# The w_out product of a two-block transformer layer as three rounded passes instead of one float32 product

## The chip, the cores and the metric

One core of one Trainium2 chip. The metric is the device time of one execution, in microseconds (us): the median of several runs.

## The reference

Two blocks follow one another on 512 tokens of width 1024, all in float32. Of the first block this case concerns its middle: four mixers (attention `a`, windowed attention `b`, a pooling mix, a long convolution) each give 256 channels, and these are joined, multiplied by `w_out` and added to the residual. Then come a norm, a router, 16 experts of which each token takes two, and the final norm of the block. The second block begins with another norm and a projection `w_in`.

```python
xl = xl + g1_l * (jnp.concatenate([a_l, b_l, p_l, h_l], axis=-1) @ lp['w_out'])
hl2 = rmsnorm(xl, lp['norm2_g']) * (1.0 + sc2_l) + sh2_l
y = moe(hl2.reshape(B * S, D), router_w, router_b, lp['moe_w1'], lp['moe_w3'], lp['moe_w2'])
xl = xl + g2_l * y.reshape(B, S, D)
...
x = rmsnorm(xl, final_g)            # end of block one
h = rms_norm(x, norm_gain[l])       # start of block two
proj = jnp.einsum('bsd,de->bse', h, w_in[l])
```

## The kernel before

The residual `xT` lies with channels on the partitions: 8 parts `k` of 128 channels, each 512 tokens wide. The joined mixers lie the same way in `mixT`, which is the first 512 columns of `hT`: parts 0 and 1 come from attention `a`, 2 and 3 from `b`, 4 and 5 from the pooling, 6 and 7 from the convolution. `arena` is one large scratch buffer whose regions change hands; `ring` has three slots of 2 MB for weights.

Every engine has its own program, written out by hand; they meet at semaphores. What PE fills and others read goes through four pairs of PSUM banks, taken in turn by *units* in one fixed order (`units_of_block_one`, `units_after_moe`). A unit names the engine that empties its banks (`act` or `dve`); PE may start a unit only once the unit four places earlier is emptied (`start_unit`, `banks_free`).

*The loop of attention b* (`turns`, L96; PE from L2851, ACT from L1239, DVE from L2036) goes through 16 pairs of query tile and head. In turn i PE transposes the probabilities of i-1 (`t`, L2865), makes the scores of i+1 (`s`, a split product in three passes) and the output of i-1 (`o`, L2602). DVE adds the bias (L1963) and takes the maximum (L1964), ACT makes the exponential (L1249) and copies the transposed probabilities (L1267), in the order exp(i+1), copy of t(i). Behind every fourth pair `ot` transposes the outputs (L2845), and ACT copies them into `mixT` (L1219). At i = 12 the outputs of attention a are transposed as well (L2882, copy L1277).

*After the loop* comes the unit `pm`: two float32 products of 512 columns for the pooling mix, which ACT scales into `mixT` (L1289). Then `w_out(j)` for j = 0 to 3 (L2890): two output parts each, for each part 8 float32 products of a 128x128 weight block by 512 columns. All float32 and rounded products of a helper are recorded at L2602 (`products`). DVE adds each part to the residual (L2072), ACT squares it (L1314). Between them stand `sr` and `rc` (small products for the router's shift), fed by 16 small copies on ACT (L1295), and the router's sums of squares (`route_sums`, L2914). ACT splits the first experts' weights into high parts (`moe_high`, L1309) and DVE makes the low parts (`moe_low`, L2064), in the gaps.

*A split product* runs in three passes: each operand x is written as a rounded copy hi (type float32r, made by ACT) and the rest lo = x - hi (made by DVE, in place of x); PE then sums w_hi·x_hi, w_hi·x_lo and w_lo·x_hi. The experts (L2992 to L2994), the second block's `w_in` (`in2_unit`, L3120 to L3122) and others are computed so already; `w_out` is not.

*Experts.* There are 17 tiles in this execution. The routing ends in a product that makes the list of tokens by tile (`list`). GpSimd gathers 128 token rows for each tile by an indirect DMA (L1011), PE transposes them (L2986), ACT and DVE split them (L1357, L2236), and PE goes through w1, w3 and, one tile behind, w2. SP loads expert weights of 2 MB each. After the first gather (`s_taken`, 16 for each) it issues w1 of tile 1, w2 of tile 0 and w3 of tile 1 (L848 to L851), and from then on each load waits until its slot has been split. ACT writes each tile's result to memory (L1341, L1343). At the end GpSimd gathers two rows for each token back (L1033).

*Final norm of block one and norm of block two.* DVE adds the experts' results (L2291), ACT squares (L1406), and PE sums the squares with two weightings: for each k and each of 4 token tiles one product with the squares as the weights and 2 columns moving (L3080), 64 in all. From the sums DVE, ACT and DVE make two factors for each token (L2303 to L1687), DVE spreads them onto diagonals (L2310) and PE broadcasts them (`n4`, `nx`).

`load(n)` on SP, for a slab of `w_in` from the fourth on (n = 22 and 23), first waits for the unit that last used its slot:

```python
if earlier and not N_BEFORE_OUT <= n < N_BEFORE_MOE + RING:
    filled(sp, last_unit[SLABS[earlier[-1]]])
```

For n = 22 that unit is `("q", 1)`, the second unit of the `w_in` product.

## Time and profile before

| what | value |
|---|---|
| median of 3 runs | 1423.01 us (1418.47 to 1431.56) |
| the profiled execution, own time | 1431.44 us |
| its span in the profile | 1429.6 us |
| PE busy | 1291.4 us, 90% of the span |
| DVE busy | 835.5 us, 58% |
| ACT busy | 572.8 us, 40% |
| mean granted clock of PE | 0.943 of full speed |

Times in the profile count from the start of the span. PE is TensorE, PEld its weight loads, DVE is VectorE, ACT is ScalarE, POOL is GpSimd, SP is SyncE. L12 is line 12 of the kernel before. A float32 product shows as two records, a rounded one as one.

### The profile page before, as it was taken

What the parts mean: (1) busy time and instruction counts of PE and PEld (TensorE: products, weight loads), DVE (VectorE), ACT (ScalarE), POOL (GpSimd) and SP (SyncE); (2) the same over time, 40 slices, a digit from 0 to 9 for tenths busy, and PEclk for the clock granted to TensorE, in tenths of its full rate; (3) what the DMA queues carried; (4) which work ended last, traced back from release to release, by engine and by line L of the source; (5) the groups of instructions that cost most, each with busy time, mean ns of one, the idle gap of its engine ahead of it and who ended that gap; (6) DMA issues with size and microseconds to landing.
All of it is one profiled execution on the core that took longest, in us unless ns stands there. A gap on an engine that the chain in (4) does not pass through costs nothing.

```text
span 1429.6 us, 16966 instructions
## 1 busy us (share of the span) xinstructions
PE 1291.4 (90%) x6478; PEld 927.3 (65%) x6478; DVE 835.5 (58%) x1241; ACT 572.8 (40%) x752; POOL 127.7 (9%) x126
## 2 busy tenths in 40 slices
PE   6999999988899899599999999589988898989796
PEld 2554456666768545478888788468867777765674
DVE  2347978736866205578888888454226456634444
ACT  1413000114545423267777777332324343334322
POOL 1100101000015000110122111100000000000000
PEclk9989999999999999699999999759998999889898
DMA  9523737565040030589999999722333454544201
GB/s 370 239 83 120 263 142 291 206 136 114 1 169 19 1 122 32 233 301 397 407 404 417 393 405 402 296 95 86 104 128 106 158 174 143 158 148 161 88 1 59
DMA packets 52838, 270.67 MB, mean 189 GB/s; under 512 B 15047, under 2 KB 22087, under 8 KB 38056
## 3 DMA queue, kind: packets, MB, share of 16 engines
q1 hardware_dynamic: 38280, 209.52, 39.7%
q0 software_dynamic: 9744, 47.19, 8.9%
q10 hardware_dynamic: 4752, 13.11, 2.3%
q8 instruction: 42, 0.69, 0.2%
q14 instruction: 20, 0.16, 0.0%
HBM read 229.42 MB, written 36.70 MB: 186 GB/s over the span
## 4 chain that ended last, share of the span: by engine, by line
PE 77%; DVE 10%; DMA 4%; ACT 4%; issue 4%; POOL 0%; SPq 0%; DVEq 0%; ACTq 0%; POOLq 0%
PE PS L2602 29%; PE PS L2992 7%; PE PS L2993 6%; PE PS L2994 6%; PE PS L3215 3%; PE PS L3216 3%; PE PS L3217 3%; PE PS L3121 2%; PE PS L3120 2%; PE PS L3122 2%; PE PS L3201 1%; PE PS L2865 1%; PE PS L2619 1%; PE PS L2986 1%; DMA arena<-stream_rows,arena 1%
## 5 line engine op out<-in xcount | busy, mean ns | idle before, releaser
L2602 PE MATMUL PS<-arena 128*128 128x64 f32 (+7 forms) x786 | 194.8, 414 | 24.6 <-DMA arena<-in_small_f_w 7.6
L1309 ACT ACTIVATE arena_r<-ring 128x2048 fp32r<-128x2048 f32 x100 | 185.9, 1910 | 18.4 <-DMA ring<-in_moe 11.8
L2602 PEld LDWEIGHTS PS<-arena 128*128 128x128 f32 (+2 forms) x786 | 119.7, 201 | 90.0 <-issue 67.6
L2602 PE MATMUL PS<-hT,ring 128*128 128x512 f32 (+1 forms) x432 | 175.1, 563 | 1.4 <-ACT hT L1289 1.4
L2064 DVE TENSOR_TENSOR arena_r<-ring,arena_r 128x2048 fp32r<-128x2048 f32 x66 | 148.2, 2287 | 21.2 <-ACT arena_r L1309 21.2
L2602 PEld LDWEIGHTS PS<-hT,ring 128*128 128x128 f32 x432 | 81.1, 190 | 92.3 <-issue 86.9
L3215 PE MATMUL PS<-arena_r 128*128 128x512 f32 x256 | 106.1, 415 | 16.7 <-DVE ring_r L2463 12.3
L2992 PE MATMUL PS<-arena_r,hT_r 128*128 128x512 f32 x272 | 112.2, 413 | 5.5 <-DVE hT_r L2236 4.9
L2993 PE MATMUL PS<-arena_r,hT_r 128*128 128x512 f32 x272 | 108.1, 398 | 0.0
L3217 PE MATMUL PS<-arena_r,ring_r 128*128 128x512 f32 x256 | 103.7, 405 | 0.0
L1160 ACT ACTIVATE arena<-PS 128x1024 f32<-128x1024 f32 (+2 forms) x31 | 28.5, 927 | 176.5 <-PE PS L2602 161.7
L2064 DVE TENSOR_TENSOR hT_r<-ring,arena_r 128x2048 fp32r<-128x2048 f32 x34 | 76.4, 2289 | 26.2 <-ACT arena_r L1309 26.1
L2463 DVE TENSOR_TENSOR ring_r<-ring,arena_r 128x1024 fp32r<-128x1024 f32 (+1 forms) x40 | 40.3, 1011 | 84.5 <-ACT arena_r L1452 83.9
L3216 PE MATMUL PS<-hT_r,arena_r 128*128 128x512 f32 x192 | 77.4, 403 | 0.0
L1773 DVE TENSOR_TENSOR arena<-arena 128x512 f32<-128x512 f32 (+2 forms) x104 | 71.9, 692 | 3.7 <-DVE arena L1815 0.2
L3215 PEld LDWEIGHTS PS<-arena_r 128*128 128x128 f32 x256 | 50.0, 195 | 35.7 <-issue 16.7
L2992 PEld LDWEIGHTS PS<-arena_r,hT_r 128*128 128x128 f32 x272 | 51.7, 190 | 21.7 <-DVE hT_r L2236 5.7
L2274 DVE TENSOR_TENSOR ring_r<-ring,arena_r 128x1024 fp32r<-128x1024 f32 x18 | 21.9, 1225 | 64.0 <-ACT arena_r L1400 64.0
L1452 ACT ACTIVATE arena_r<-ring 128x1024 fp32r<-128x1024 f32 (+1 forms) x40 | 35.3, 884 | 58.2 <-PE PS L3217 54.0
L2993 PEld LDWEIGHTS PS<-arena_r,hT_r 128*128 128x128 f32 x272 | 51.8, 190 | 10.4
L3217 PEld LDWEIGHTS PS<-arena_r,ring_r 128*128 128x128 f32 x256 | 50.0, 195 | 11.8
L2992 PE MATMUL PS<-arena_r 128*128 128x512 f32 x136 | 54.4, 400 | 2.8 <-DVE arena_r L2229 2.8
(428 smaller groups left out, 2308.0 us busy)
## 6 DMA issues: line engine op xcount, KB each, us to landing
ring<-in_moe SPq DMA_DIRECT2D x51, 2048.0 KB, 10.9
ring<-in_slabs SPq DMA_DIRECT2D x27, 2048.0 KB, 10.3
ring<-in_slabs SPq DMA_DIRECT2D x9, 1024.0 KB, 6.0
y_rows<-arena ACTq DMA_DIRECT2D x17, 512.0 KB, 10.0
ssm_scratch<-arena POOLq DMA_DIRECT2D x4, 1152.0 KB, 6.2
arena<-ssm_scratch POOLq DMA_DIRECT2D x4, 1152.0 KB, 9.0
arena<-in_tab_fwd SPq DMA_DIRECT2D x2, 2048.0 KB, 15.0
ssm_scratch<-arena POOLq DMA_DIRECT2D x4, 1024.0 KB, 10.3
```

Source lines behind the costliest of these rows:

```text
L1309: nc.scalar.activation(rounded(moe_w_hi[n][:, cols]), ring[:, n, cols], ACT.Copy).then_inc(s_moe_hi[n], 1)
L1452: nc.scalar.activation(rounded(w_hi[:, n % 2, 0:w.shape[1]]), w, ACT.Copy).then_inc(s_w_hi, 1)
L1773: then(nc.vector.tensor_tensor(out, x, y, op))
L2064: nc.vector.tensor_tensor(rounded(moe_w_lo[n][:, cols]), ring[:, n, cols], as_float(moe_w_hi[n][:, cols]), ALU.subtract).then_inc(s_moe_lo ...
L2463: nc.vector.tensor_tensor(rounded(w), w, as_float(w_hi[:, n % 2, 0:w.shape[1]]), ALU.subtract).then_inc(s_w_lo, 1)
L2602: ins = nc.tensor.matmul(out, lhsT, rhs, start=(n == 0), stop=(n == len(pairs) - 1))
L2992: nc.tensor.matmul(out, rounded(x_hi), rounded(w_hi_), start=first, stop=False)
L2993: nc.tensor.matmul(out, rounded(x_lo), rounded(w_hi_), start=False, stop=False)
L2994: return nc.tensor.matmul(out, rounded(x_hi), rounded(w_lo_), start=False, stop=last)
L3215: nc.tensor.matmul(out, w_h, x_h, start=(k == 0), stop=False)
L3216: nc.tensor.matmul(out, w_h, x_l, start=False, stop=False)
L3217: ins = nc.tensor.matmul(out, w_l, x_h, start=False, stop=(k == last))
```

## The change

It computes `w_out` as a split product in three passes. The four joined mixers are split in eight parts: ACT makes the high parts of 6, 7, 0 and 1 and of the first weight chunk inside the loop of attention b (`during_b`), the others after it; DVE follows with the low parts. The weights go in 8 chunks of 128 output channels through three buffers. The unit `pm` moves into the loop at i = 14. Other edits: SP waits for the second gather, not the first, before the loads of L848 to L851; SP waits for the last gather of results before the fourth and fifth slab of `w_in`; the first split of w3 moves on ACT behind the copies of the normed rows; at the end of the experts ACT copies the last tile's transposed gates ahead of the second but last result; the one-hot operands of `list` are rounded; the two sums of squares are made with 32-column weights and 512 columns moving, the roots taken from PSUM on 64 rows and transposed. Scratch regions of squares move, and semaphores are renamed.

```diff
@@ -111,6 +111,8 @@
             yield ("ot", i // HEADS - 1)
+        if a == "b" and i == 14:
+            yield ("pm",)
@@ -118,6 +120,8 @@
         return ("a", "ot"), "act"
+    if kind == "pm":
+        return ("pm",), "act"
@@ -147,7 +151,6 @@
             u += [((a, "ot", QT - 1), "act")]
-    u += [(("pm",), "act")]
@@ -239,7 +242,7 @@
     u = [(("y_tr", j), "dve") for j in range(4)]
-    u += [(("n3", 0), "dve"), (("n3", 1), "dve"), (("n4",), "dve"), (("nx",), "dve")]
+    u += [(("n3",), "act"), (("nt",), "dve"), (("n4",), "dve"), (("nx",), "dve")]
@@ -364,6 +367,21 @@
         o_a2 = region(R_HY, [QT, 256])
+        WO_CHUNKS, MIX_PARTS = 8, 8
+        mix_hi = region(R_HY + 1024, [KD, T])
+        wo_hi = [region(start, [KD, P]) for start in (R_HY, 0, 1024)]
+        def wo_weights(n):
+            w = slab(("w_out", n // 4)).rearrange("p (k c) -> p k c", k=KD)
+            return w[:, :, P * (n % 4):P * (n % 4) + P]
+        def wo_chunk_done(eng, n):
+            if n % 2:
+                filled(eng, ("wo", n // 2))
+            else:
+                eng.wait_ge(s_chunk_a, n // 2 + 1)
@@ -843,7 +862,7 @@
                 sp.dma_start(ring[:, 2], moe_d[bass.ds(3 * e + 2, 1)].rearrange("a p c -> p (a c)")).then_inc(s_moe_w[2], 16)
-            sp.wait_ge(s_taken, 16)
+            sp.wait_ge(s_taken, 32)
@@ -863,6 +882,7 @@
             sp.wait_ge(s_moe_y, tiles)
+            sp.wait_ge(s_back[QT - 1], 32)
@@ -1221,6 +1241,30 @@
                                      ACT.Copy).then_inc(s_act_read, 1)
+            def mix_high(k):
+                nc.scalar.activation(rounded(mix_hi[:, k]), mixT[:, k], ACT.Copy).then_inc(s_op_hi, 1)
+            def wo_high(n):
+                slab_here(act, ("w_out", n // 4))
+                if n >= 3:
+                    wo_chunk_done(act, n - 3)
+                nc.scalar.activation(rounded(wo_hi[n % 3]), wo_weights(n), ACT.Copy).then_inc(s_w_a_hi, 1)
+            def during_b(i):
+                if i in (9, 10):
+                    act.wait_ge(s_gate, 4)
+                    mix_high(i - 3)
+                elif i == 11:
+                    act.wait_ge(s_pool_d, 4)
+                    wo_high(0)
+                elif i in (13, 14):
+                    read(act, ("a", "ot"))
+                    mix_high(i - 13)
@@ -1271,6 +1315,13 @@
                             high_b(i)
+                        else:
+                            during_b(i)
+                    elif turn[0] == "pm":
+                        filled(act, key)
+                        for g in range(2):
+                            ins = nc.scalar.activation(mixT[:, 4 + g], bank(key, g), ACT.Copy, scale=V("pool_scale", g, g + 1))
+                        ins.then_inc(s_act_read, 1)
@@ -1283,21 +1334,22 @@
                     out_tr(a, QT - 1)
-            key = ("pm",)
-            filled(act, key)
-            for g in range(2):
-                ins = nc.scalar.activation(mixT[:, 4 + g], bank(key, g), ACT.Copy, scale=V("pool_scale", g, g + 1))
-            ins.then_inc(s_act_read, 1)
+            read(act, ("b", "ot", QT - 1))
+            for k in range(2, 6):
+                mix_high(k)
+            wo_high(1)
+            wo_high(2)
...
                 ins.then_inc(s_diags, 1)
+            wo_high(3)
...
             copy_unit(("rc",), rt_const, bank(("rc",), 0)[:, 0:EXPERTS])
+            wo_high(4)
@@ -1312,8 +1364,12 @@
                 nc.scalar.activation(sq_2[:, k], xT[:, k], ACT.Square).then_inc(s_sq, 1)
-                if k in (3, 5):
-                    moe_high((k - 3) // 2, 0, False)
+                if k == 1:
+                    wo_high(5)
+                    wo_high(6)
+                elif k == 3:
+                    wo_high(7)
+                    moe_high(0, 0, False)
@@ -1325,6 +1381,7 @@
                 copy_unit(("h_tr", t), h_rows[:, t], both(("h_tr", t)), rt_rstd[:, t:t + 1])
+            moe_high(1, 0, False)
@@ -1385,8 +1442,8 @@
                 nc.scalar.activation(rounded(moe_w_hi[0][:, cols]), ring[:, 0, cols], ACT.Copy).then_inc(s_moe_hi[2], 1)
+            gT_high(tiles - 1)
             moe_y_out(tiles - 2)
-            gT_high(tiles - 1)
...
-            root(4, nst[:])
+            act.wait_ge(s_gsq, 2)
+            filled(act, ("n3",))
+            nc.scalar.activation(root_rows[0:64], bank(("n3",), 0)[0:64], ACT.Sqrt, scale=1.0 / D,
+                                 bias=eps_n[0:64]).then_inc(s_act_read, 1)
...
                 act.wait_ge(s_h2, k + 1)
@@ -2034,6 +2094,18 @@
                                                 in1=V("norm2_g"), op0=ALU.add, op1=ALU.mult))
+            def wo_low(n):
+                dve.wait_ge(s_w_a_hi, n + 1)
+                w = wo_weights(n)
+                nc.vector.tensor_tensor(rounded(w), w, as_float(wo_hi[n % 3]), ALU.subtract).then_inc(s_w_a_lo, 1)
+            def mix_low(part):
+                dve.wait_ge(s_op_hi, part)
+                k = (6, 7, 0, 1, 2, 3, 4, 5)[part - 1]
+                nc.vector.tensor_tensor(rounded(mixT[:, k]), mixT[:, k], as_float(mix_hi[:, k]), ALU.subtract).then_inc(s_op_lo, 1)
@@ -2044,6 +2116,14 @@
                 norm_a(i)
+                if i == 12:
+                    wo_low(0)
+                elif i in (11, 13, 14, 15):
+                    mix_low({11: 1, 13: 2, 14: 3, 15: 4}[i])
+            for part in range(5, 9):
+                mix_low(part)
+            for n in range(1, 3):
+                wo_low(n)
@@ -2064,6 +2144,7 @@
                                             ALU.subtract).then_inc(s_moe_lo[n], 1)
+            wo_low(3)
@@ -2077,6 +2158,9 @@
                         ins.then_inc(s_x1, 1)
+                if j < 2:
+                    wo_low(2 * j + 4)
+                    wo_low(2 * j + 5)
@@ -2250,8 +2334,10 @@
                 nc.vector.tensor_tensor(moe_g, moe_s, PS[:, 1, :], ALU.mult).then_inc(s_moe_g, 1)
-            nc.vector.memset(gsq[:, :, 0:1], 1.0).then_inc(s_gsq, 1)
-            nc.vector.tensor_tensor(gsq[:, :, 1], V("final_g"), V("final_g"), ALU.mult).then_inc(s_gsq, 1)
+            then(nc.vector.tensor_tensor(gsq[:], V("final_g"), V("final_g"), ALU.mult))
+            nc.vector.tensor_scalar(gsq_32, gsq[:, :, None].broadcast_to([P, KD, 32]), EPS, None, ALU.add).then_inc(s_gsq, 1)
+            nc.vector.memset(eps_n[0:32], EPS * EPS)
+            nc.vector.memset(eps_n[32:64], EPS).then_inc(s_gsq, 1)
@@ -2296,16 +2382,11 @@
                         ins.then_inc(s_x2, 1)
-            for half in range(2):
-                key, tiles_of = ("n3", half), slice(2 * half, 2 * half + 2)
-                filled(dve, key)
-                sums = PS[:, 2 * U.slot(key):2 * U.slot(key) + 2, 0:2]
-                then(nc.vector.tensor_scalar(nst[:, 1, tiles_of], sums[:, :, 0], 1.0 / D, EPS, ALU.mult, ALU.add))
-                nc.vector.scalar_tensor_tensor(out=nst[:, 0, tiles_of], in0=nst[:, 1, tiles_of], scalar=EPS * D,
-                                               in1=sums[:, :, 1], op0=ALU.mult, op1=ALU.add).then_inc(s_dve_read, 1)
-                read(dve, key)
-            nc.vector.tensor_scalar(nst[:, 0], nst[:, 0], 1.0 / D, None, ALU.mult).then_inc(s_mean, 1)
-            inverse(4, nst[:])
+            key = ("nt",)
+            filled(dve, key)
+            nc.vector.reciprocal(nst[:], bank(key, 0)[:, 0:64 * QT].rearrange("p (t a c) -> p a t c", a=2, c=32)[:, :, :, 0]
+                                 ).then_inc(s_dve_read, 1)
+            read(dve, key)
@@ -2882,29 +2963,34 @@
                         ins.then_inc(s_filled, 1)
+                    elif turn[0] == "pm":
+                        start_unit(key)
+                        pe.wait_ge(s_pool_d, 4)
+                        for g in range(2):
+                            products(bank(key, g), [(pool_w[:, g], pool_d[:, g])], last=(g == 1))
...
                     out_tr(a, QT - 1)
-            key = ("pm",)
-            start_unit(key)
-            pe.wait_ge(s_pool_d, 4)
-            for g in range(2):
-                products(bank(key, g), [(pool_w[:, g], pool_d[:, g])], last=(g == 1))
...
                 start_unit(key)
-                if j == 0:
-                    read(pe, ("pm",))
-                    pe.wait_ge(s_gate, 4)
-                slab_here(pe, ("w_out", j // 2))
-                w = slab(("w_out", j // 2)).rearrange("p (k c) -> p k c", k=KD)
                 for c in range(2):
-                    col = 256 * (j % 2) + P * c
-                    products(bank(key, c), [(w[:, k, col:col + P], mixT[:, k]) for k in range(KD)], last=(c == 1))
+                    n = 2 * j + c
+                    hi, lo = wo_hi[n % 3], wo_weights(n)
+                    first, then_ = (6, 7, 0, 1), (2, 3, 4, 5)
+                    passes = [[(w, x, k) for k in ks] for w, x, ks in ((hi, mix_hi, first), (hi, mixT, first), (hi, mix_hi, then_),
+                                                                      (hi, mixT, then_), (lo, mix_hi, first + then_))]
+                    pe.wait_ge(s_w_a_hi, n + 1)
+                    for m, (w, x, k) in enumerate(sum(passes, [])):
+                        if n == 0 and m in (0, 4, 8, 12):
+                            pe.wait_ge(s_op_lo if m % 8 else s_op_hi, 4 if m < 8 else 8)
+                        if m == 2 * KD:
+                            pe.wait_ge(s_w_a_lo, n + 1)
+                        ins = nc.tensor.matmul(bank(key, c), rounded(w[:, k]), rounded(x[:, k]), start=(m == 0), stop=(m == 3 * KD - 1))
+                    ins.then_inc(s_filled if c else s_chunk_a, 1)
@@ -3071,16 +3157,19 @@
                 ins.then_inc(s_filled, 1)
-            for half in range(2):
-                start_unit(("n3", half))
-            pe.wait_ge(s_gsq, 2)
+            start_unit(("n3",))
+            pe.wait_ge(s_gsq, 1)
...
                 pe.wait_ge(s_sq, 3 * KD + k + 1)
-                for t in range(QT):
-                    ins = nc.tensor.matmul(bank(("n3", t // 2), t % 2)[:, 0:2], sq[:, k, P * t:P * t + P], gsq[:, k],
-                                           start=(k == 0), stop=(k == KD - 1))
-                    if k == KD - 1 and t % 2:
-                        ins.then_inc(s_filled, 1)
+                for n, w in enumerate((gsq_32[:, k], ones[:, 0:32])):
+                    ins = nc.tensor.matmul(bank(("n3",), 0)[32 * n:32 * n + 32, :], w, sq[:, k, 0:T], start=(k == 0), stop=(k == KD - 1))
+            ins.then_inc(s_filled, 1)
+            key = ("nt",)
+            start_unit(key)
+            read(pe, ("n3",))
+            for t in range(QT):
+                ins = nc.tensor.transpose(bank(key, 0)[:, 64 * t:64 * t + 64], root_rows[0:64, P * t:P * t + P], ident[0:64, 0:64])
+            ins.then_inc(s_filled, 1)
...
```

## Rows read from the trace of the kernel before

**Rows 1.** The page, part 4: the chain that ended last, shares of the span by line
```profile
PE PS L2602 29%; PE PS L2992 7%; PE PS L2993 6%; PE PS L2994 6%; PE PS L3215 3%; PE PS L3216 3%; PE PS L3217 3%; PE PS L3121 2%; PE PS L3120 2%; PE PS L3122 2%; PE PS L3201 1%; PE PS L2865 1%; PE PS L2619 1%; PE PS L2986 1%; DMA arena<-stream_rows,arena 1%
```

**Rows 2.** Stretches: us, busy (count) of PE, PEld, DVE, ACT, POOL; granted clock; DMA share; GB/s
```profile
core 0: us, PE busy (x) PEld busy (x) DVE busy (x) ACT busy (x) POOL busy (x), PEclk, DMA share, GB/s
486.00:488.00 2.00, 2.00 (x5) 0.97 (x6) 0.76 (x5) 0.38 (x1) 0.00 (x0) 0.54 0.02 4
613.00:903.00 290.00, 289.35 (x1344) 235.13 (x1345) 250.28 (x143) 222.70 (x158) 46.44 (x30) 1.00 0.97 391
948.00:950.00 2.00, 2.00 (x11) 2.00 (x11) 0.00 (x0) 0.00 (x0) 0.00 (x0) 0.50 0.00 0
973.20:1062.50 89.30, 89.30 (x389) 72.37 (x388) 26.61 (x28) 26.33 (x28) 1.06 (x2) 1.00 0.26 84
```

**Rows 3.** Timeline of PE, end of loop b to w_out: start, us, line, count, idle before
```profile
465.05 1.52 PE L2602 MATMUL PS<-arena 128*128 128x64 f32 x12 [0.28 <-ACT arena L1267]
...
480.44 1.52 PE L2602 MATMUL PS<-arena 128*128 128x64 f32 x12 [1.46 <-ACT arena L1267]
...
486.15 3.58 PE L2602 MATMUL PS<-arena 128*128 128x512 f32 x4
491.13 13.97 PE L2602 MATMUL PS<-hT,ring 128*128 128x512 f32 x32 [1.40 <-ACT hT L1289]
```

**Rows 4.** Timeline of ACT, one turn of loop b, and the evacuation of pm
```profile
464.11 0.80 ACT L1267 ACTIVATE arena<-PS 128x768 f32<-128x768 f32 x1
...
489.76 1.26 ACT L1289 ACTIVATE hT<-PS,vec 128x512 f32<-128x512 f32 x2 [3.03 <-PE PS L2602]
```

**Rows 5.** Groups by shape on ACT and DVE, whole run: count, busy us, mean ns
```profile
L1400 ACT ACTIVATE arena_r<-ring 128x1024 fp32r<-128x1024 f32 x18 | 18.8, 1055 | 32.0 <-PE PS L3122 23.3 <-PE PS L3105 8.1 <-ACT arena L1341 0.6
...
L1410 ACT ACTIVATE arena_r<-hT 128x512 fp32r<-128x512 f32 x8 | 5.1, 632 | 4.3 <-DVE hT L2315 4.1
...
L2274 DVE TENSOR_TENSOR ring_r<-ring,arena_r 128x1024 fp32r<-128x1024 f32 x18 | 21.9, 1225 | 64.0 <-ACT arena_r L1400 64.0
```

**Rows 6.** The chain in order of time, 440 to 1120 us: start, us, what
```profile
577.33 3.59 PE PS L2602 x16
...
590.95 11.46 DMA arena<-stream_rows,arena
...
941.31 13.80 PE PS L3080 x64
```

**Rows 7.** DMA issues in short stretches: KB each, us from issue to landing
```profile
arena<-stream_rows,arena POOLq DMA_INDIRECT x1, 5.6
...
ring<-in_moe SPq DMA_DIRECT2D x1, 2048.0 KB, 17.8
...
ring<-in_moe SPq DMA_DIRECT2D x1, 2048.0 KB, 7.7
```

**Rows 8.** Timelines of SP, ACT and PE around the second tile
```profile
588.43 0.37 SPq L848 DMA_DIRECT2D ring<-in_moe  x1
...
599.98 3.70 ACT L1309 ACTIVATE arena_r<-ring 128x2048 fp32r<-128x2048 f32 x2
...
613.04 0.50 PE L2992 MATMUL PS<-arena_r,hT_r 128*128 128x512 f32 x1 [2.43 <-DVE hT_r L2236]
```

**Rows 9.** Timeline of ACT and PE around the last expert_out
```profile
905.09 0.60 ACT L1348 ACTIVATE arena_r<-PS 128x512 fp32r<-128x512 f32 x1 [0.56 <-ACT arena L1341]
...
906.63 0.79 PE L2992 MATMUL PS<-arena_r 128*128 128x512 f32 x1 [2.83 <-DVE arena_r L2229]
```

**Rows 10.** Timelines and groups around the two norms' sums
```profile
939.04 1.34 ACT L1406 ACTIVATE arena<-xT 128x512 f32<-128x512 f32 x2 [19.10 <-DVE xT L2291]
...
956.28 1.29 DVE L2310 TENSOR_TENSOR arena<-ident,nst 128x512 f32<-128x512 f32 x2
...
558.31 0.44 PE L2955 MATMUL PS<-ident,arena 64*128 64x64 f32 x4 [0.87 <-DVE arena L2086]
...
L1318 ACT ACTIVATE arena<-PS,arena 32x512 f32<-32x512 f32 x1 | 0.7, 680 | 0.1
```

49 lines of the change are left out of this document (25 added, 24 removed).

## The prediction, made before the changed kernel ran

> **What bounds the kernel now.** I read the page's chain first, then stretches with their granted clock, then the timeline of each place that the diff touches. The chain is mostly PE, and its largest line is L2602, the helper through which the float32 products go, w_out's among them [rows 1]. The changed places are therefore on the path, or hold it up. Four matter.
>
> The tail of loop b and w_out: PE makes pm in 3.58 us at about half clock, waits for ACT's two copies and starts w_out at 491.13, in units of 13.97 us [rows 2, 3]. The list: 16 short records take 3.59 us [rows 6]. The experts: PE is busy 289.35 of 290 us at full clock with DMA at 0.97, so inside the loop there is nothing to win and little to spare; only its start (a second gather of 11.46 us, a restart of PE at 613.04) and its end (906.63) are loose [rows 2, 6, 8, 9]. The norm sums: 64 products with 2 columns take 13.80 us while the clock stands at 0.50 [rows 2, 6].
>
> **The product itself.** Before: 4 x 13.97 = 55.9 us [rows 3]. After: 8 chunks x 8 blocks x 3 = 192 passes of 512 columns. The w_in product makes 16 chunks of 24 passes in 89.30 us; about 0.6 us of that are transposes, so a pass takes 88.7/384 = 0.231 us [rows 2]. 192 x 0.231 = 44.4 us: 11.5 us less. It is on the path, since nothing behind it can start before the residual parts.
>
> **pm moved.** From 486.15 to 491.13 PE does nothing but pm and wait: 5.0 us go from the tail [rows 3], since the first eight passes need only parts that the loop has already split. In the loop pm costs PE 3.58/2 = 1.8 us at full clock; its copies (1.26 us on ACT [rows 4]) stand beside t(14) and replace a wait of 1.46 us before o(14) [rows 3]. If that cover is missing they cost 1.3 us more.
>
> **Splits in the loop.** ACT gets four copies of 0.63 us and one of 1.05 us [rows 5]. They stand between an exponential and the copy of t(i), for which PE waits: copy at 464.11, PE at 465.05 after 0.28 us idle [rows 3, 4]. So they are not free. The one at i = 10 costs 0.6 us. The one at i = 11 is swallowed, since the exponential of that turn was not delayed by the earlier shift. The weight chunk at i = 12 costs 1.05 us. Those at i = 14 and 15 lie under pm and under a wait. Together 1.7 us; between 0 and 3.6 us (all five exposed). Queued behind them on ACT are the copies of t(i), and behind these PE. DVE's low parts come after its output of the turn, in a wait for scores.
>
> **The start of w_out.** After the last ot ACT must copy it (0.38 us in the profile) and split four parts, 2.5 us. PE meanwhile makes eight passes. pm ran at 3.58/8 = 0.45 us a pass at that place, and the tail's waits stay as they are, so I count the eight at half clock: 8 x (0.45 - 0.23) = 1.8 us lost, and the four parts arrive just in time. At full clock they would take 1.8 us and PE would wait some 1.1 us: nearly the same.
>
> **The feed of the later chunks.** High part 1.05 us, low part 1.23 us [rows 5], chunk 24 x 0.231 = 5.5 us, three buffers. Chunk n+3's high part waits for chunk n, so it has two chunks, 11 us, to be ready. Queued in front of wo_high(3) are the 16 diagonal copies (4.9 us), in front of wo_high(4) sr's and rc's copies. By my order of time, with w_out starting at 0, wo_low(3) ends near 16 and chunk 3 starts near 22; chunk 4 starts near 29, its low part ends near 19; chunk 7's low part waits for chunk 4 and ends near 37, chunk 7 starts near 48. Nothing waits, and the first w1 split comes behind wo_high(7) with its load then landed. If all of the feed were exposed: 8 x 2.3 = 18 us.
>
> Net of these parts: 11.5 + 5.0 - 1.8 - 1.7 - 1.8 = 11.2 us.
>
> **The list.** Rounded operands make 8 passes of 16 records: 3.59/2 = 1.8 us less [rows 6], and the first gather waits for it. No row shows a rounded product of 24 columns; bounds 0 and 2.5 us.
>
> **Loads after the second gather.** Alone, a gather lands in 5.6 us; the second, beside three loads, took 11.46 [rows 6, 7]. PE waited 3.0 us for it, so this wait goes. What is late next is w1 of tile 1: the loads leave near 597.3 instead of 588.43 [rows 8]. A load with the queue to itself lands in 7.7 us [rows 7], so at 605.0. Then half a high split (1.9), two low splits (4.5), the gate product (0.7) and the low part of the taken rows (1.2) follow on ACT and DVE, and PE restarts at 613.4 against 613.04 [rows 8]. I take 0. Bounds: 3 us won if loads and gather are each faster; 4 us lost if w1 takes as long as the row allows, 599.98 - 588.43 = 11.5 us [rows 8]. By tile 2 the delay is gone, since DMA stands nearly idle between 609 and 626 in the profile. The Trainium skill says (DMA: Bandwidth & Descriptors, "Queues, rings and completion order") that completion is not in order of issue within one issuing engine. The last of the three loads landed after 17.8 us [rows 7]; if w1 landed only then, PE would restart some 10 us later. The trace speaks for order of issue: w1's split started with no wait at 599.98.
>
> **The end of the experts.** gT_high now precedes the result copy and can start 1.2 us sooner than 905.09 [rows 9], but PE also needs the copy (1.0 us) behind it: PE starts at about 905.7 instead of 906.63, 0.9 us. It runs its first passes at 0.43 us there; should the shorter gap keep the clock up, 3 us more. Bounds 0 and 4.
>
> **Norm sums.** Now 16 float32 products of 512 columns, two side by side for each k. Per k: 4 passes, 1.8 us at half clock (0.45 each), 0.92 at full. The first square is ready near 939.7 [rows 10]. Elsewhere wide products bring the full clock after some 3.5 us (pm at half clock, w_out behind it at full) [rows 2, 3]; so two k at 1.8 and six at 0.92 end at 948.8. Squares come every 0.75 us and do not hold it. Then a root (0.68), four transposes (0.44), a reciprocal (0.2): diagonals at 950.3 instead of 956.28 [rows 10], 6.0 us. If the clock stays low: 8 x 1.8, ending at 954.1, and 0.7 us are won. Best case 7.5. The Trainium skill (TensorE: Matmul & The Clock Gate, "What's actually happening") says that the array is throttled by default and that being busy releases it. The row disagrees for the old sums: PE busy 2.00 of 2.00 us at 0.50 [rows 2]. [...]
>
> **At nothing.** The first w3 split moves to ACT behind the row copies, where ACT is idle from 574 to 590, and DVE wants it near 580; without that cover 3.7 us, still before w3's use at 604. SP's wait for the result gathers delays nothing: the two loads behind it already wait for ("q", 1), long after. So that edit does not do what it says, and the result gathers stay as they are.
>
> **Sum.** 11.2 + 1.8 + 0 + 0.9 + 6.0 = 19.9 us. The profiled execution: 1431.4 - 19.9 = 1411.5. It lies at the upper end of the three runs; their median is 1423.0, so the time is 1403. A measurement tells about 1% (14 us) from no change, so "faster" begins below 1409.
>
> **Rivals.**
> - *All loose ends fall well* (clock kept at the expert end, splits hidden, gather gain kept): 19.9 + 1.7 + 1.5 + 3 + 3 + 0.5, about 30 us, 1393. For it: each wait is short. Against: they are independent. Chance 0.12.
> - *The clock stays low in the norm sums, and w1 comes late*: 5.3 + 4 us less gain, about 1412. For it: the clock stood at 0.50 for this whole stretch; against: pm. 0.14 for either of them in full.
> - *The w_out feed is exposed*: PE waits for each chunk's split in the hand-written queues of ACT and DVE: 18 us back, 1421. Against: 11 us of lead. 0.05.
> - *Slower: the experts become paced by DMA.* DMA is at 0.97 [rows 2], and the loads start 9 us later. If the lead is never regained, every tile waits. It decides from 19.9/15 = 1.3 us a tile; at 2 us for 15 tiles it costs 30 us, 1433. Against: the idle DMA stretch at the start, and a split loop that needs less than the 18.1 us of a tile. 0.04.
>
> My forecast itself, within 6 us: 0.65. It leaves 1397 to 1409. Down to 1391 most of the first rival is in, up to 1413 the second; outside remain the last two and the tails. Faster: 0.65 + 0.12 and about half of the second, 0.84; the same: 0.12; slower: 0.04.
>
> **What would show it.** w_out chunks of 5.5 us with no wait for ACT or DVE but in the first; pm at half its time in the loop; o(10) and o(12) later by 0.6 and 1.0 us; the second gather near 5.6 us, PE restarting within 1 us of the old distance; wide norm sums of about 9 us with the clock rising within them. Chunks above 6 us, a tile above 18.3 us, or norm sums above 13 us would make the forecast wrong.

## The result, and the profile after

The changed kernel took 1417.63 us, the median of 20 runs (1411.66 to 1429.75); 20 runs of the kernel before (the three of the table among them) gave 1428.04 (1418.47 to 1438.4). The ratio is 0.995 (0.9929 to 0.9972). That is 7 us less by the ratio and 10.4 by the medians: a gain, but one within 1%. The forecast was 1403 us, within 1397 to 1409, or 1391 to 1413 with its nearest rivals; the time lies above both ranges. "Faster" was to begin below 1409 and had a chance of 0.84; what came is what the forecast called "the same", at 0.12. The profiled execution took 1416.47 us with a span of 1414.6 (before 1431.44 and 1429.6).

The chain has w_out in a line of its own now: L2992 holds 3%, and the float32 helper, which is L2683 in the new file, 26% instead of 29% [rows 1]. The page of the changed kernel, part 4, shares of the span by line:

```profile
PE PS L2683 26%; PE PS L3078 7%; PE PS L3079 6%; PE PS L3080 6%; PE PS L2992 3%; PE PS L3304 3%; PE PS L3305 3%; PE PS L3306 3%; PE PS L3210 2%; PE PS L3209 2%; PE PS L3211 2%; PE PS L2946 1%; PE PS L3290 1%; PE PS L2700 1%; PE PS L3072 1%
```

A chain of shares doesn't say where the rest of the gain went, so I laid the two profiled executions side by side, from marker to marker (lengths in us; a marker is the start of the row named):

| stretch | before | after | gain | forecast |
|---|---|---|---|---|
| loop b: first output transpose, ot(0), to the last, ot(3) | 34.36 | 44.35 | -10.0 | -3.5 |
| tail and w_out: ot(3) to the row sums behind w_out's last chunk | 67.91 | 54.29 | +13.6 | +14.7 |
| list: to the first tile's row transposes | 33.91 | 32.13 | +1.8 | +1.8 |
| start of the experts: to the first gate transposes | 31.02 | 32.91 | -1.9 | 0 |
| experts: first to last gate transposes | 284.47 | 283.52 | +1.0 | 0 |
| end of the experts: to the last result copy | 12.19 | 12.36 | -0.2 | +0.9 |
| last result copy to the first square | 23.64 | 23.50 | +0.1 | 0 |
| norm sums: first square to the diagonals | 17.24 | 11.39 | +5.9 | +6.0 |
| together | | | +10.3 | +19.9 |

The two executions lie 15.0 us apart. The missing 4.7 are outside the table, 1.6 ahead of ot(0) and 3.1 behind the diagonals; such stretches differ from one execution to the next by more than that (below). What has to be explained is 10.3 where 19.9 were forecast, and two thirds of the gap stand in the first line: loop b became 10 us longer.

The timeline of PE in loop b of the changed kernel, 455 to 500 us (start, length, line, count, idle before and what ended it):

```profile
463.92 1.52 PE L2683 MATMUL PS<-arena 128*128 128x64 f32 x12 [0.79 <-ACT arena L1311]
...
473.02 1.67 PE L2683 MATMUL PS<-arena 128*128 128x64 f32 x12 [1.20 <-ACT arena L1311]
474.48 1.49 PE L2946 MATMUL PS<-ident,arena 128*128 128x128 f32 x6
475.90 2.29 PE L2683 MATMUL PS<-arena_r,hT_r 64*128 64x512 f32 x6
478.12 6.34 PE L2683 MATMUL PS<-arena 128*128 128x64 f32 x16
...
486.61 1.60 PE L2683 MATMUL PS<-arena 128*128 128x64 f32 x12 [1.41 <-ACT arena L1311]
...
490.91 2.79 PE L2683 MATMUL PS<-arena 128*128 128x64 f32 x12 [0.99 <-ACT arena L1311]
494.25 0.66 PE L2926 MATMUL PS<-ident,post 128*128 128x128 f32 x2 [0.54 <-DVE post L2054]
494.56 2.05 PE L2992 MATMUL PS<-arena_r 128*128 128x512 f32 x4
...
498.12 1.11 PE L2992 MATMUL PS<-arena_r 128*128 128x512 f32 x4
```

The two waits are the ones forecast: 0.79 us ahead of o(10), 1.20 ahead of o(12), where the same place had 0.25 to 0.28 before [rows 3]. What the forecast did not have is the column of lengths behind the second one. Six transposes (L2946) take 1.49 us there and 0.82 in an earlier turn (465.50); the group of 16, which is o(13) and pm together, takes 6.34. The stretches of the changed kernel around it (us, busy and count of PE, PEld, DVE, ACT, POOL; granted clock; DMA share; GB/s):

```profile
440.00:473.00 33.00, 30.10 (x213) 25.83 (x211) 22.00 (x39) 18.29 (x33) 11.94 (x9) 1.00 0.00 1
473.00:476.00 3.00, 2.98 (x19) 2.67 (x19) 2.04 (x5) 0.99 (x2) 0.00 (x0) 0.71 0.00 0
476.00:484.00 8.00, 8.00 (x22) 5.56 (x23) 2.78 (x6) 2.32 (x4) 0.00 (x0) 0.50 0.00 0
484.00:488.00 4.00, 2.59 (x19) 2.13 (x18) 0.00 (x0) 2.48 (x4) 0.00 (x0) 0.93 0.00 0
488.00:498.00 10.00, 8.47 (x32) 7.26 (x32) 3.22 (x8) 4.22 (x8) 0.00 (x0) 0.50 0.01 2
```

The granted clock is 1.00, which is 2.4 GHz, until 473, and falls to 0.50, which is 1.2 GHz, within three microseconds of the wait of 1.20. It stays there through eight microseconds in which PE is busy without a break, and again in the tail. In the kernel before the loop ran at 1.00 to its last turn, and the clock was low only behind it, in the tail [rows 2].

Who made PE wait is seen on ACT (same columns as for PE, timeline of ACT of the changed kernel):

```profile
469.33 0.90 ACT L1293 ACTIVATE arena<-PS,stat 128x768 f32<-128x768 f32 x1 [1.95 <-DVE stat L2024]
...
470.22 1.05 ACT L1254 ACTIVATE arena_r<-ring 128x1024 fp32r<-128x1024 f32 x1
471.17 1.01 ACT L1328 ACTIVATE hT<-PS 128x1024 f32<-128x1024 f32 x1
472.07 0.80 ACT L1311 ACTIVATE arena<-PS 128x768 f32<-128x768 f32 x1
```

L1254 is the rounded copy of w_out's first chunk. It stands between the exponential and the copy of the transposed probabilities (L1311), and so does a copy that this one turn has anyway, that of attention a's transposed outputs (L1328, which was L1277 before). With that copy alone PE waited 0.25 us here; with both it waits 1.20.

At the start of the experts the chain of the changed kernel, 560 to 960 us, reads (start, length, what):

```profile
575.37 5.25 DMA arena<-stream_rows,arena
580.67 1.98 PE PS L3072 x8
...
583.90 4.02 DMA arena<-stream_rows,arena
588.68 8.56 DMA ring<-in_moe
597.26 1.92 ACT arena_r L1361
...
601.42 2.28 DVE arena_r L2144
...
604.30 1.15 DVE hT_r L2320
...
899.41 10.03 DMA y_rows<-arena
...
933.73 7.71 PE PS L3165 x32
941.51 1.28 ACT L1466
942.81 0.69 ACT rstd L1466
```

The second gather now lands in 4.02 us instead of 11.46 [rows 6], as asked for; but the chain goes on through the load of w1, which left only at 588.68. While w1 was loaded and split PE stood idle for 5.74 us, and it restarted at 605.49 (timeline of PE of the changed kernel):

```profile
605.49 0.79 PE L3078 MATMUL PS<-arena_r,hT_r 128*128 128x512 f32 x1 [5.74 <-DVE hT_r L2320]
```

The granted clock is at 0.50 there (a stretch of the changed kernel, in the columns of the stretches above):

```profile
605.50:608.00 2.50, 2.50 (x6) 2.02 (x7) 0.00 (x0) 0.00 (x0) 0.00 (x0) 0.50 0.94 380
```

The end of the experts runs through a store of 10.03 us. The norm sums take 7.71 us instead of 13.80 [rows 6].

### The profile page after: what moved, and what is told of

Its sections match the earlier page's. It is cut to its first block, busy times and chain, and to the rows that moved or that the text cites. A ratio compares the mean times of both kernels' runs of the same rounds, so it can differ in the third digit from the quotient of the medians.

```text
span 1414.6 us, 17056 instructions
## 1 busy us (share of the span) xinstructions
PE 1273.6 (90%) x6506; PEld 930.1 (66%) x6506; DVE 849.2 (60%) x1254; ACT 585.3 (41%) x768; POOL 126.4 (9%) x126
## 4 chain that ended last, share of the span: by engine, by line
PE 77%; DVE 9%; DMA 5%; ACT 5%; issue 4%; POOL 1%; SPq 0%; POOLq 0%; DVEq 0%; ACTq 0%
PE PS L2683 26%; PE PS L3078 7%; PE PS L3079 6%; PE PS L3080 6%; PE PS L2992 3%; PE PS L3304 3%; PE PS L3305 3%; PE PS L3306 3%; PE PS L3210 2%; PE PS L3209 2%; PE PS L3211 2%; PE PS L2946 1%; PE PS L3290 1%; PE PS L2700 1%; PE PS L3072 1%
## 5 line engine op out<-in xcount | busy, mean ns | idle before, releaser
L2683 PE MATMUL PS<-arena 128*128 128x64 f32 (+6 forms) x770 | 189.0, 412 | 21.3 <-ACT arena L1311 8.9
L2683 PEld LDWEIGHTS PS<-arena 128*128 128x128 f32 (+2 forms) x770 | 116.8, 200 | 84.6 <-issue 61.5
L3078 PE MATMUL PS<-arena_r,hT_r 128*128 128x512 f32 x272 | 113.0, 416 | 8.2 <-DVE hT_r L2320 8.2
L2683 PE MATMUL PS<-hT,ring 128*128 128x512 f32 (+1 forms) x304 | 119.2, 550 | 0.0
L3304 PE MATMUL PS<-arena_r 128*128 128x512 f32 x256 | 105.1, 410 | 15.5 <-DVE ring_r L2544 11.3
L3079 PE MATMUL PS<-arena_r,hT_r 128*128 128x512 f32 x272 | 109.3, 402 | 0.0
L2683 PEld LDWEIGHTS PS<-hT,ring 128*128 128x128 f32 x304 | 57.1, 190 | 59.0 <-issue 56.6
L3080 PE MATMUL PS<-arena_r,hT_r 128*128 128x512 f32 x136 | 55.3, 407 | 0.0
```

Source lines behind the costliest of these rows:

```text
L2683: ins = nc.tensor.matmul(out, lhsT, rhs, start=(n == 0), stop=(n == len(pairs) - 1))
L3078: nc.tensor.matmul(out, rounded(x_hi), rounded(w_hi_), start=first, stop=False)
L3079: nc.tensor.matmul(out, rounded(x_lo), rounded(w_hi_), start=False, stop=False)
L3080: return nc.tensor.matmul(out, rounded(x_hi), rounded(w_lo_), start=False, stop=last)
L3304: nc.tensor.matmul(out, w_h, x_h, start=(k == 0), stop=False)
```

## The experiments

Each experiment edits the changed kernel, most in one place (x5 in two, x8 in three), and the measure is the stretch of the table in which the edit stands; whole times of single runs are told only where they matter. The first run is the changed kernel itself, on the chip and in the session of the next three.

**The changed kernel once more (x0_again).**

> The changed kernel once more, unaltered. From the transposes of ot(0) to those of ot(3) it took 44.4 us, against 34.4 before the change; 3.5 us more were forecast. Theory A (the splits in front of the copy of t(i) open a gap on PE of 1.2 us at i = 12, and the clock falls behind it): the fall comes at the same place again, near 474, and the stretch takes 43 to 45 us. Theory B (the fall was chance in one execution): the clock stays at 1.00 to about 486 and the stretch takes about 38 us.

Measured: loop b 44.21 us (44.35), ot(0) to the end of w_out 98.59 (98.64), start of the experts 33.16 (32.91), end 11.99 (12.36), norm sums 11.46 (11.39). In these two executions a stretch repeats within 0.4 us. Over all the runs below, where no edit touches them, loop b stays within 0.5 us (44.21 to 44.72 in six traces) and the start of the experts within 0.7 (32.72 to 33.37 in nine), but the list varies by 2.3 us (30.95 to 33.23), the end of the experts by 1.4 (11.20 to 12.57) and the norm sums by 2.0 (10.80 to 12.84). So single runs tell differences above 0.7 us in the first two stretches, and only larger ones in the others. The time of this run was 1414.37.

**The splits behind the copy that PE waits for (x1_after_copy).**

```
     # ACT, loop b: exponential | copy of probT (the "t" turn) | "o" turn
     (copy of probT, L1311)
+    if a == "b":
+        during_b(i)
...
-    else:
-        during_b(i)
```

> The five splits of the loop stand behind the copy of t(i) on ACT, where ACT waits 1.6 to 2.2 us for the maximum, instead of in front of it. Theory A: PE sees no new gap, the clock holds until pm is done, ot(0) to ot(3) takes 36 to 37 us (34.4 and pm at 1.8), w_out's chunks are unchanged, the kernel is 6 to 8 us faster than the changed one (ratio to the kernel before about 0.988). Theory C (pm's two wide products in the loop bring the clock down or are the cost themselves): the stretch stays at 43 us or more, with the clock at 0.50 from pm on, and the time stays as it is.

Measured: loop b 37.85 us, to the end of w_out 92.61 (98.64), a median of 1409.04 us in 4 runs and a ratio of 0.989 (0.982 to 0.996) to the kernel before. The splits themselves are all still there, in the same turns; one place further on in ACT's queue they cost PE nothing, and the loss from them was 6.5 us, not 1.7. (Theory A had named 36 to 37 us; the clock of the tail, below, took the rest.) The timeline of PE of this kernel:

```profile
473.54 1.52 PE L2683 MATMUL PS<-arena 128*128 128x64 f32 x12 [0.25 <-ACT arena L1311]
476.90 3.33 PE L2683 MATMUL PS<-arena 128*128 128x64 f32 x16
482.38 1.52 PE L2683 MATMUL PS<-arena 128*128 128x64 f32 x12 [1.49 <-ACT arena L1311]
486.20 2.80 PE L2683 MATMUL PS<-arena 128*128 128x64 f32 x12 [0.99 <-ACT arena L1311]
```

The wait ahead of o(12) is back at 0.25, and the group of 16 takes 3.33 us. The clock now falls only behind the 1.49 us wait of the tail, and o(15) pays 1.3 us for it.

**pm back in the tail (x2_pm_tail).** The rival theory for the long group was pm itself, since it is new in the loop.

```
     # order of the units
-    if a == "b" and i == 14: yield ("pm",)
...
+    u += [(("pm",), "act")]          # behind ot(3)
```

> pm stands behind the loop again, the splits stay in front of the copy of t(i). Theory A: the gap of 1.2 us at i = 12 is there, the clock falls behind it though pm is gone; ot(0) to ot(3) takes 39 to 41 us. Theory C: without pm in the loop the clock holds to about 486, the stretch takes 36 us (34.4 and 1.7 of gaps). In both pm costs 3.5 us at the tail, and w_out's first eight passes run beside its copies.

Measured: loop b 42.24 us, to the end of w_out 100.45. Without pm in it the loop is still 7.9 us longer than before, and the wait of 1.20 us ahead of o(12), which ends at 477.79, is followed by the half clock again: 0.69 from 477 to 482 and 0.50 from there. So pm isn't what brings the clock down. The loop came out longer than the 39 to 41 us of theory A, since the clock stayed at 0.50 through all its last turns. Moved back it costs 1.8 us more over the whole stretch.

**No splits in the loop at all (x3_splits_late).**

```
-    else:
-        during_b(i)
...
+    for i in (9, 10, 11, 13, 14):    # after the last ot, ahead of mix_high(2)
+        during_b(i)
```

(DVE's low parts follow them.)

> All splits stand behind the loop, pm stays in it. Theory A: no new gap before pm, so ot(0) to ot(3) takes 36 to 37 us; w_out starts 2 to 4 us after ot(3), since ACT must first make four parts and a weight chunk (0.4 + 2.5 + 1.05 us) and DVE the low parts; up to w_out's end it is 3 to 5 us shorter than the changed kernel. Theory C: the stretch stays at 43 us or more.

Measured: loop b 36.16 us, which is 34.36 + 1.80: pm costs what was forecast, to the hundredth. But w_out then waits 3.58 us for its first parts, and to its end it is 94.58, two microseconds worse than with the splits in the loop but behind the copy. That is what they are worth in the loop in these two runs, in both of which the eight first passes ran at half clock.

**Which of the five splits it is (x9_weights_in_front, x10_parts_in_front).** In the first only the weight chunk (1.05 us) stays ahead of the copy, in the second only the four parts (0.62 us each).

```
x9:   +  if a == "b" and i not in (11,): during_b(i)            # behind the copy
      -  else:                                      # at the "o" turn
      +  elif i in (11,):
x10:  +  if a == "b" and i not in (9, 10, 13, 14): during_b(i)
      -  else:
      +  elif i in (9, 10, 13, 14):
```

> Of the five splits only the weight chunk at i = 12 (1.05 us) stands in front of the copy, the four of 0.63 us behind it. Theory A (one gap of about 1.2 us on PE is enough for the clock to fall): ot(0) to ot(3) takes 42 to 44 us, the clock at 0.50 from about i = 13. Theory D (only several gaps in a row do it, the sum counts): the clock holds, 39 us.

> The reverse: the four parts stand in front of the copy, the weight chunk behind it. Theory A: gaps of at most 0.8 us, the clock holds, 38 to 39 us. Theory D: the clock falls here too, 42 us or more.

Measured: 41.61 and 36.48 us. The timeline of PE with the weight chunk in front:

```profile
477.41 1.52 PE L2685 MATMUL PS<-arena 128*128 128x64 f32 x12 [1.19 <-ACT arena L1311]
482.26 6.35 PE L2685 MATMUL PS<-arena 128*128 128x64 f32 x16
```

and with the four parts in front:

```profile
464.86 1.52 PE L2685 MATMUL PS<-arena 128*128 128x64 f32 x12 [0.80 <-ACT arena L1311]
...
476.38 3.32 PE L2685 MATMUL PS<-arena 128*128 128x64 f32 x16
```

One instruction carries most of it. Where no split delays PE and the clock holds, the loop takes 36.16 us (x3 and x8). The part at i = 10 costs 0.55 us of waiting (0.80 against 0.25), of which the stage loses 0.3. The weight chunk costs 0.94 us of waiting (1.19 against 0.25) and lengthens the loop by 5.4 us, three of them in the group of 16 alone. (Theory A had 42 to 44 us here, and 38 to 39 for x10; both came out shorter.) With all five in front, the changed kernel loses 8.2: of what is left, 2.2 us are a second fall of the clock in the last turns, which x9 doesn't have and x1 has without the wait of 1.2 us (ot(2) to ot(3) is 6.25 us in the changed kernel, 4.10 in x9, 5.79 in x1). Over all profiles of this study: with the wait of 1.2 us ahead of o(12) the clock fell right behind it in 8 of 8 (the changed kernel, x0, x2, x4 to x7, x9), without it the loop kept 1.00 through o(13) in 5 of 5 (before, x1, x3, x8, x10).

**The loads behind the first gather again (x4_first_gather).**

```
-    sp.wait_ge(s_taken, 32)
+    sp.wait_ge(s_taken, 16)
```

> Only SP's wait is undone: the three loads leave after the first gather again. Measured from the transposes of the first gathered tile to the first transposes of gates it was 31.0 us before the change, 32.9 and 33.2 in two executions with it. Theory A (w1 of tile 1 lands late, PE idles 5.7 us and restarts at half clock): 31.0 us, the second gather back at 11 us, PE waits 3 us for it. Theory B (the late loads cost nothing, the 1.9 us come from elsewhere): 32.9 us as with the change.

Measured: start of the experts 29.80 us (32.91). The chain of this kernel:

```profile
576.25 11.71 DMA arena<-stream_rows,arena
588.00 1.10 PE PS L3072 x8
```

The second gather takes 11.71 us again and PE waits 2.24 us for it. Yet the stage is 3.1 us shorter than with the wait in place (31.0 were expected): the weights leave 7.9 us earlier, 5.4 us behind the first gather's issue instead of 13.3, and PE's idle time is split in two waits, 2.24 and 2.43 us, instead of one of 5.74. PE restarts only 0.7 us sooner (24.10 us behind the first transposes, for 24.82), but at full clock, and is then 5.70 us from the gates instead of 8.09:

```profile
597.11 0.50 PE L3078 MATMUL PS<-arena_r,hT_r 128*128 128x512 f32 x1 [2.43 <-DVE hT_r L2320]
```

The wait bought a fast gather with a late w1, and that was a bad exchange, mostly through the clock. This run took 1398.79 us, but some 7 us of that belong to no edit: its ot(0) stands at 442.7 us, that of the changed kernel at 449.9.

**Only w1 ahead of the second gather (x7_w1_first).**

```
-    sp.wait_ge(s_taken, 32)
+    sp.wait_ge(s_taken, 16)
     (load of w1)
+    sp.wait_ge(s_taken, 32)
     (loads of w2 and w3)
```

> Only w1 of tile 1 leaves after the first gather, w2 and w3 wait for the second. Theory A: the second gather then shares DMA with one load and lands after 6 to 9 us, w1 lands 8 to 9 us after its issue, before PE needs it; PE waits 1 us or less for the gather; from the transposes of the first tile to the first gates 29 to 31 us. Rival: the gather is as slow beside one load as beside three (11 us), 31 us or more; or w3 of tile 1 now comes last and PE waits for it, 32 us.

Measured: 27.23 us, 5.7 less than the changed kernel and 3.8 less than the one before, a larger gain than I had expected. The timelines of SP, POOL and PE:

```profile
581.27 0.37 SPq L867 DMA_DIRECT2D ring<-in_moe  x1
583.80 0.98 POOL L1032 DMA_INDIRECT arena<-stream_rows,arena  x1 [0.81 <-POOL arena L1042]
590.17 0.34 SPq L869 DMA_DIRECT2D ring<-in_moe  x1
...
602.11 0.50 PE L3079 MATMUL PS<-arena_r,hT_r 128*128 128x512 f32 x1 [2.43 <-DVE hT_r L2321]
```

w1 leaves 7.4 us sooner. PE doesn't wait for the gather (its transposes follow a pass without a gap, at 593.05), and it restarts with the short wait of 2.43 us that the first tile has too. It also restarts at a full clock, at 0.23 us a pass (0.43 in the changed kernel, where it had stood idle for 5.7 us).

**The order at the end of the experts undone (x5_undo_order).**

```
-    sp.wait_ge(s_back[QT - 1], 32)
...
     moe_y_out(tiles - 2)
+    gT_high(tiles - 1)
     moe_y_out(tiles - 1)
```

(gT_high stood ahead of both result copies.)

> Two edits undone that should be worth nothing: SP's wait for the last result gather, and ACT's order at the end of the experts. From the last transposes of gates to the copy of the last result it was 12.2 us before the change, 12.4 and 12.0 with it. Theory A (the last copy waits for the store of the result before it, which takes 10 us): within 0.6 us of 12.2 again. Theory B (PE's earlier start counts): 13 us, 0.9 more. The result gathers: 14 to 15 us from first issue to last landing in any case, since the two loads behind SP's wait come later anyway; if the wait did something, they would take 2 us or more longer.

Measured: end of the experts 12.45 us (12.36), result copy to first square 23.35 (23.50). Neither part shows a difference, though for the first, with 11.20 to 12.57 in the other kernels with the new order, one of some tenths can't be excluded. The timeline of ACT says why. The changed kernel:

```profile
897.73 0.60 ACT L1405 ACTIVATE arena_r<-PS 128x512 fp32r<-128x512 f32 x1 [2.45 <-PE PS L3094]
898.22 1.02 ACT L1398 ACTIVATE arena<-PS 128x1024 f32<-128x1024 f32 x1
899.41 0.34 ACTq L1400 DMA_DIRECT2D y_rows<-arena  x1
909.46 1.02 ACT L1398 ACTIVATE arena<-PS 128x1024 f32<-128x1024 f32 x1 [10.21 <-DMA y_rows<-arena]
```

PE does start its last product sooner: 899.37 is 2.27 us behind the gate transposes, where 906.63 [rows 9] was 3.42 us behind them. But there is one buffer for results, so the last copy waits for the store of the copy before it, which left at 899.41 and took 10.03 us. Before, PE ended that wait (9.72 us, to 915.40, the store having landed at 914.78); now the store does.

**The table of the root loaded early (x6_root_table).**

```
     act.wait_ge(s_gsq, 2)
+    nc.scalar.activation(stat[0:64, 7, 7:8], eps_n[0:64], ACT.Sqrt)
     filled(act, ("n3",))
```

> One more square root of a single column ahead of ACT's wait for the sums, so that the table for roots is loaded before them. With the change the load of 1.28 us stood between the sums and the root, from the first square to the diagonals it was 11.4 to 11.5 us. Theory: 10.1 to 10.3 us. Rival: the table is not needed sooner, something else on ACT or PE ends last: 11.4 us.

Measured: norm sums 10.08 us (11.39, and 10.80 to 12.84 in the kernels without this edit; x8 below repeats it with 10.09). The timeline of ACT:

```profile
939.74 1.28 ACT L1465 ACT_TABLE_LOAD   x1
941.03 0.20 ACT L1465 ACTIVATE stat<-stat 64x1 f32<-64x1 f32 x1
942.24 0.68 ACT L1467 ACTIVATE rstd<-PS,stat 64x512 f32<-64x512 f32 x1 [1.01 <-PE PS L3166]
```

The load of 1.28 us now lies beside the last sums. PE, which waits 0.86 us for the root instead of 2.20, also makes the four broadcasts behind it in 1.95 us instead of 3.65.

**The three together (x8_three_mended): x1, x7 and x6 in one kernel.**

> Three edits on the changed kernel together: the loop's splits behind the copy of t(i), w1 of tile 1 alone after the first gather, the root's table loaded early. Alone they shortened their stretches by 6.5 us (loop), 5.3 us (start of the experts) and 2.2 us (norms to the first product of w_in). If they add up: 14 us less than the changed kernel, a ratio to the kernel before of about 0.983. Rival: the earlier end of one stage is lost in the next (a load then comes late): 0.988 or above.

Measured: 1397.46 us in 6 runs (1392.19 to 1404.73) against 1428.77 for the kernel before in 11, a ratio of 0.9804 (0.975 to 0.9858). It beats the kernel before, and, as its interval lies below the changed kernel's (0.9929 to 0.9972), that one too, though the two were not run side by side. Loop b 36.16, to the end of w_out 89.82, start of the experts 27.59, norm sums 10.09: 8.8 + 5.3 + 1.3 us below the changed kernel, 15.4 in all. The medians of the two kernels lie 20.2 us apart. Of the difference 0.8 us is the faster broadcast behind the diagonals; the other 4 us are in no stretch that these edits touch, and the two medians are from different chips. The timeline of PE in its tail:

```profile
479.52 3.32 PE L2685 MATMUL PS<-arena 128*128 128x64 f32 x16
...
484.99 1.52 PE L2685 MATMUL PS<-arena 128*128 128x64 f32 x12 [1.49 <-ACT arena L1312]
...
488.39 1.52 PE L2685 MATMUL PS<-arena 128*128 128x64 f32 x12 [0.99 <-ACT arena L1312]
...
490.62 1.18 PE L2994 MATMUL PS<-arena_r 128*128 128x512 f32 x4
...
493.56 1.19 PE L2994 MATMUL PS<-arena_r 128*128 128x512 f32 x4 [0.83 <-ACT arena_r L1247]
```

Here the clock stayed at 1.00 through the whole tail, the first eight passes took half their time, and PE then waited 0.83 us for the four parts that ACT splits after the last ot: the two cases that the prediction called nearly the same. The waits of 1.49 and 0.99 us are those of x1, behind the first of which it fell. x10 held its clock here too. So the fall in the tail is not settled by these waits alone; what decides between the two stays open.

## Why the prediction was wrong

The forecast held in most of its terms and failed in one, with two small misses beside it.

- **Failed: "Splits in the loop", "together 1.7 us".** The waits were right: 0.79 us ahead of o(10), 1.20 ahead of o(12), and against the 0.25 that x1 has there this is 1.5 us in all. The splits at 14 and 15 cost nothing, as said. But the step counted a wait on PE at its own length. Behind the wait of 1.20 us the clock fell, and that was the larger part: of the loop's 10.0 us, 1.8 are pm (x3), 1.5 the waits, and the other 6.7 the half clock. About 5.0 of these go with the splits (6.5 us between the changed kernel and x1, less the 1.5 of waits), and about 1.7 are a fall in the last turns that x1 has as well (37.85 against 36.16), so they are not shown to come from the splits. x9 and x10 put the first fall on one instruction, the weight chunk. The sentence "between 0 and 3.6 us (all five exposed)" excluded the truth, because its upper end was a sum of durations. I had read the clock of the tail [rows 2], so the way in which waits and clock hang together was in view; I never asked it of the stretch in which I was adding a wait. The Trainium skill has the shape of this (TensorE: Matmul & The Clock Gate, "A second HAM failure mode: psum-queue depth-cycling"): idle moments between groups of matmuls can be frequent enough that the clock goes down and up. The traces here agree that short waits can do it, with 18 of the 22 us from 476 to 498 at 0.50; what they add is that one wait of 1.20 us (x9: 1.19) was followed by the fall, where the page speaks of frequent ones.
- **Right: the product, pm, the start of w_out, the feed.** The three-pass product needs 11.34 us for a pair of chunks (524.01 to 535.35 in the timeline of PE), where a unit of the same size took 13.97 [rows 3]. Forecast were 11.09: 0.25 a pair, 1.0 us in all four, is nearly the whole miss of the tail's line (13.6 for 14.7). No chunk but the first waited, so the rival of an exposed feed is out. The first eight passes ran at 0.45 us, as taken (494.56 to 498.12).
- **Right: the list**, 1.8 us. The product itself takes 1.85 us in the timeline of PE, where it took 3.59 [rows 6]; the stretch around it varies by more than that between runs.
- **Missed by size: "Loads after the second gather", "I take 0", bounds -3 and +4.** It lost 1.9 us against before and 3.1 against the same kernel without the wait (x4). The restart itself was as forecast: 24.82 us behind the first transposes, where it was 25.32 before (613.04 - 587.72) and 25.7 were worked out. w1 left 1.6 us sooner than thought and took 8.56 us from issue instead of 7.7; why, stays open, as in x4, with the same two loads behind it, it took 7.70. The loss stands behind the restart: PE, idle for 5.7 us, went on at 0.43 us a pass, and the gates came 8.09 us later instead of 5.70. The forecast had no term for that; it is the error of the loop a second time. The step's reading that DMA stands nearly idle between 609 and 626 was wrong: its share in the trace of before is 0.94 from 609 to 614, 0.08 from 614.5 to 618.5 and 0.85 from there to 626. Nothing came of it, as the experts took no longer. The prediction weighed a rule of the Trainium skill (DMA: Bandwidth & Descriptors, "Queues, rings and completion order"), that completion isn't in order of issue; the trace spoke for order again, with the three loads landing at 597.24, 602.80 and 608.33.
- **Missed: "The end of the experts", 0.9 us.** PE started 1.15 us sooner, where 0.9 were worked out, but nothing that can be told came of it: the store and the single result buffer were the next to be late. The step named PE's releasers and stopped at PE.
- **Right: the norm sums**, 5.9 us for 6.0. The sums took 7.71 us where about 9.1 were counted, since the clock rose sooner than the 3.5 us that the step took from pm: records fall from 1.03 us to 0.59 at the third pair, 1.5 us after the start. The 1.4 us won there went to a table load of 1.28 us ahead of the root, for which the step had no term (it priced the root alone, at 0.68). Two errors cancelled, which is luck, and x6 shows the one by removing it. The Trainium skill asks that activations be grouped by the set of their functions (ScalarE: Activation LUTs, "Table sets: the hidden batching unit"); with one root in this place there is nothing to group, and the row says that putting the load ahead of the wait is enough.
- **Right: at nothing.** The wait for the result gathers delays nothing (x5: 23.35 and 23.50 us).
- **The base.** The forecast subtracted 19.9 us from 1423.0, the median of three runs. Twenty runs gave 1428.0. From that base the same sum gives 1408: 5 us of the 14.6 between forecast and time are the base's, the other 9.6 are the gain that failed to come.

Of the rivals, none was the cause. The nearest, a low clock in the norm sums and a late w1, was half right about w1 and put the low clock in the wrong stage. The experts did not become paced by DMA: 283.52 us for 284.47.

## What to carry to other kernels

A wait that an edit adds to TensorE is not worth its own length: in a stretch of small products, 0.94 us more of waiting in one turn made it 5.4 us longer (x9), most of that through the clock, so look for the granted clock of the stretch that receives the edit, and put the new work behind the copy that TensorE waits for. When a DMA is held back so that another lands sooner, ask who needs the one held back and at what clock that engine will restart, and try holding back only the part that nobody needs yet (w2 and w3, not w1). And when a releaser is moved forward, follow the row to the engine or the store behind it: a single result buffer took back the gain at the end of the experts.

## What was not expected of the hardware

- The clock fell behind a single wait of 1.2 us in 8 of 8 profiles, with PE busy 30.10 of the 33 us before it, and then stayed at 0.50 from 476 to 484, in which PE was busy without a break. In the tail the waits of 1.49 and 0.99 us were followed by a fall behind the first in x1, by one only at 484.8, in a longer wait, in x3, and by none in x8 and x10; before, with 1.46 and 0.99, it fell at 486. And at the restart of the experts a wait of 2.43 us left the clock full (x4, x7, x8), where one of 5.74 did not. So the length of the last wait alone does not tell.
- A store of 512 KB took 10.03 us from issue, beside loads of 2 MB, the last issued 1.4 us before it; the next, issued at 910.65 with no load beside it, took 2.63.
- One load of three, first in the queue, took 8.56 us in the changed kernel and 7.70 in x4; the second gather took 4.02 us with no load beside it, 6.35 with one (x7) and 11.71 with three (x4).
- Stretches that no edit touches differ between executions: ot(0) stood anywhere from 442.7 to 454.7 us. That is as much as all of this change, so a single time of one kernel says little, and distances between markers in one stage say more.
